# Delta rule block inverses moved from TensorE to GpSimd, with the chunk products four chunks ahead

## What is computed

```
k_beta = k * beta[..., None]; v_beta = v * beta[..., None]
lower = where(strict, einsum('cd,sd->cs', k_beta, k) * decay, 0)
system = lower + eye(C)
sol = triangular_solve(system, [v_beta, k_beta * exp(g)], lower=True)   # u, w
a_qk = where(causal, einsum('cd,sd->cs', q, k) * decay, 0)
step: v_new = u - w @ state
      o = q_dec @ state + a_qk @ v_new
      state = state * exp(g_last) + k_dec.T @ v_new
```

## Time and profile before

| | us |
|---|---|
| median of 3 runs | 2552.06 |
| lowest and highest of the 3 | 2546.36, 2552.57 |
| profiled execution, its own time | 2544.92 |
| its span | 2543.2 |
| where the mix stage lies in the span, about | 697 to 1597 |

### The profile page before, as it was taken

The page is one execution under the profiler, slowest core; times in us unless marked ns, Lnnn a source line. Parts: engine busy times, 40 slices in busy tenths (PEclk is TensorE's granted clock), DMA queues, the critical chain, the costliest instruction groups (busy, mean ns, idle before and its releaser), DMA issues. The chain is left out here.

```text
span 2543.2 us, 47637 instructions
## 1 busy us (share of the span) xinstructions
PE 2318.0 (91%) x17494; PEld 1332.5 (52%) x17495; DVE 1083.7 (43%) x2488; ACT 907.2 (36%) x2283; POOL 389.5 (15%) x630
## 2 busy tenths in 40 slices
PE   6999999999688999999999998799966999999990
PEld 2545545455356666666666666355543444444440
DVE  2434334333346666666666665123344222222223
ACT  2263462633635555555555544111110111111112
POOL 1000000000110000000000000233321222222224
PEclk9999999999879999999999998899987999999995
DMA  9222121111263213211222103733311879999787
GB/s 337 74 66 72 53 79 44 59 59 36 80 171 105 77 54 95 84 55 66 70 70 81 41 27 150 261 120 124 132 67 46 244 210 306 275 322 302 219 238 289
DMA packets 187895, 334.49 MB, mean 132 GB/s; under 512 B 19723, under 2 KB 119718, under 8 KB 184502
## 3 DMA queue, kind: packets, MB, share of 16 engines
q1 hardware_dynamic: 173878, 281.51, 32.4%
q0 software_dynamic: 13824, 50.34, 8.0%
HBM read 242.36 MB, written 89.44 MB: 130 GB/s over the span
## 5 line engine op out<-in xcount | busy, mean ns | idle before, releaser
L706 PE MATMUL pV<-mod_rows_then_work,w_in_sb 128*128 128x512 f32 x768 | 340.1, 596 | 4.3 <-DMA w_in_sb<-in_w_in_dram 4.3
L2077 PE MATMUL hidden_ps<-w,keys_values_then_all 128*128 x752 | 331.6, 594 | 1.1 <-SPq L1949 1.1
L1145 ACT ACTIVATE probs<-scores,neg_max 128x512 f32<-128x512 f32 (+3 forms) x320 | 199.6, 624 | 336.2 <-DVE neg_max L1274 218.5
L1428 PE MATMUL scores<-keys_values_then_all,queries 96*128 96x512 f32 (+3 forms) x640 | 306.9, 563 | 7.2 <-DMA keys_values_then_all<-kp_d 7.2
L2077 PEld LDWEIGHTS hidden_ps<-w,keys_values_then_all 128*128 128x128 f32 x752 | 143.2, 191 | 181.7 <-issue 181.7
L706 PEld LDWEIGHTS pV<-mod_rows_then_work,w_in_sb 128*128 128x128 f32 x768 | 144.4, 191 | 177.2 <-issue 176.4
L1726 PE MATMUL out_ps<-keys_values_then_all 128*128 128x512 f32 x512 | 225.5, 599 | 2.8 <-ACT keys_values_then_all L1591 2.8
L1433 PE MATMUL bank<-ident,probs 128*128 128x128 f32 x1088 | 184.5, 285 | 1.5 <-ACT probs L1145 1.3
L2007 ACT ACTIVATE keys_values_then_all<-hidden_ps 128x256 f32<-128x256 f32 x47 | 18.0, 384 | 455.7 <-PE hidden_ps L2077 455.7
L1274 DVE TENSOR_REDUCE neg_max<-scores 128x1 f32<-128x512 f32 x192 | 132.3, 689 | 111.1 <-PE scores L1428 110.1
L1445 PE MATMUL outT_ps<-probs_T,keys_values_then_all 128*64 128x128 f32 x2176 | 157.8, 284 | 21.6 <-issue 17.6
(11 more groups left out here) (368 smaller groups left out, 3338.0 us busy)
## 6 DMA issues: line engine op xcount, KB each, us to landing
w<-in_w_dram SPq DMA_DIRECT2D x64, 1024.0 KB, 10.1
w_sb<-in_w_dram SPq DMA_DIRECT2D x32, 1024.0 KB, 13.9
w_mod_rows<-in_w_mod_dram SPq DMA_DIRECT2D x16, 1024.0 KB, 4.7
kqv<-qkv_d SPq DMA_DIRECT2D x16, 768.0 KB, 4.3
mod_rows_then_work<-in_w_mod_dram SPq DMA_DIRECT2D x4, 2048.0 KB, 14.7
x_in<-in_x_dram SPq DMA_DIRECT2D x16, 512.0 KB, 4.7
qkv_d<-l_out SPq DMA_DIRECT2D x32, 256.0 KB, 2.3
keys_values_then_all<-y_d SPq DMA_DIRECT2D x16, 512.0 KB, 4.9
```

Of the source, the lines that this page charges most:

```text
L706: last = pe.matmul(pV[n % 2][:], win[:, k, QKV0 + c * P:QKV0 + (c + 1) * P], hT[:, s % 2, k, :], start=(k == 0), stop=(k == ND - 1))
L1145: act.activation(prob[:, e, 0:w].rearrange("p t k -> p (t k)"), pS[e][:, 0:w * P], ACT.Exp, scale=-1.0, bias=nmin[:, i % 2, h, b:b + 1], a ...
L1428: pe.matmul(pS[e][:, 0:w * P], qT[:, i % 2, slot(h)], kT[:, 4 * b:4 * b + w, slot(h), :], start=True, stop=True).then_inc(s_ready, 1)
L2077: last = pe.matmul(pH[par][:], xT[par][:, k], m.w13[:, ds(slot, 1), k].rearrange("p s n -> p (s n)"), start=(k == 0), stop=(k == ND - 1))
```

## The change

The four doubling levels go. In their place GpSimd inverts the 32x32 blocks by forward substitution. The four blocks of each of four heads of two chunks make 32 blocks; each lies on one of the 32 partitions 96 to 127 (in a part of the key buffer that is not used there), row after row in the free dimension. For each column j there is one product of (31 - j) x (j + 1) elements into `outer` and one subtraction from the block of the same size, each waited for before the next: 62 instructions, and two memsets and one transposing copy, for two chunks. They are cut into 16 pieces, steps I, spread over two turns.

The blocks get there by memory: K and KA now write `lt_new` and `at_new`, which SyncE stores (`store_products`), and the blocks are loaded again, a block to a partition (`load_blocks`). At IS the inverses are stored, at L they are loaded into `U`, `Wh` and `Wb`, with `lt` and `at` of that chunk. K and KA run four chunks ahead of the recurrence, with a load `load_kk` of keys and queries alone (512 KB) in one buffer, and `load_kq` loads all of it again for the recurrence. Of the inverse TensorE keeps Y 1, WU 1, Y 2 and WU 2, which are the former 5 and 6. Gates have two buffers in place of three. The block masks (15 GpSimd instructions in the projection and two VectorE reductions at its end) go.

```diff
-    for c in range(-2, NT):
-        n, d = c + 1, c + 2
...
-        steps += [(0.7, ("W0", n)), (0.8, ("Y", n, 1))] * prep
...
+    for c in range(-AHEAD, NT):
+        n, a, d = c + 1, c + AHEAD, c + AHEAD + 1
+        first, prep, rec = a < NT, 0 <= n < NT, c >= 0
+        turn = []
+        turn += [(1.0, ("K", a)), (0.5, ("KA", a))] * first
+        turn += [(0.45, ("VT", c)), (0.45, ("KD", c)), (1.0, ("KS", c)), (0.7, ("QS", c)), (0.85, ("TR", c))] * rec
+        turn += [(0.8, ("Y", n, 1))] * prep
...
+        turn += [(0.5, ("WU", n, 2))] * prep
+        turn += [(0.0, ("G", d))] * (d < NT)
+        turn += [(0.9, ("M", k)) for k in MOD_AT.get(c, ())[-1:]]
+        turn += [(0.0, ("O2", c))] * rec
+        g, half = (c + 3) // BATCH, (c + 3) % BATCH
+        if 0 <= g < NT // BATCH:
+            pieces = [(0.8 if c < 0 else 0.0, ("I", g, k)) for k in range(half * PIECES // 2, (half + 1) * PIECES // 2)]
...
+            turn += [(0.0, ("IS", g))] * half
+        turn += [(0.0, ("L", c + 2))] * (0 <= c + 2 < NT)
+        steps += turn
+    order = [("G", 0), ("K", 0), ("KA", 0), ("G", 1), ("S", 0, 0), ("X", 0, 0), ("S", 0, 1), ("X", 0, 1)]
...
+            def load_blocks(c):
+                wait(lt_stored, 16 * (c + 1))
+                wait(inv_ready, c // BATCH)
+                for q in range(4):
+                    at_row = (c % BATCH * 4 + q) * GH
+                    sp.dma_start(Ab[at_row:at_row + GH], m.a_d[c * P + BL * q:c * P + BL * (q + 1), :].rearrange(
+                        "j (h r i) -> h r j i", h=GH, r=4)[:, q]).then_inc(block_loaded, 16)
...
+            load_kk(0)
...
+            load_kq(0)
             load_kq(1)
             load_gate(0)
-            load_gate(1)
...
+                if kind == "K":
+                    if n + 1 < NT:
+                        wait(kk_ready, n + 1)
+                        load_kk(n + 1)
...
+                elif kind == "IS":
+                    wait(inv_ready, n + 1)
+                    sp.dma_start(m.inv_d[n * (P - QK):(n + 1) * (P - QK), :], both_T).then_inc(inv_stored, 16)
+                elif kind == "L":
+                    load_inverses(n)
...
+            def then(ins):
+                done[0] += 1
+                ins.then_inc(inv_step, 1)
+                pool.wait_ge(inv_step, done[0])
+
+            def invert(g, piece):
...
+                    pool.wait_ge(block_loaded, 16 * 4 * BATCH * (g + 1))
+                for j in range(piece * BL // PIECES, (piece + 1) * BL // PIECES):
+                    below, upto = BL - 1 - j, j + 1
+                    if below:
+                        prod = outer[:, 0:below * upto].rearrange("p (i c) -> p i c", i=below)
+                        then(pool.tensor_tensor(prod, Ab[:, j, j + 1:].unsqueeze(2).to_broadcast([n, below, upto]),
+                                                Tb[:, j:j + 1, 0:upto].to_broadcast([n, below, upto]), ALU.mult))
+                        then(pool.tensor_tensor(Tb[:, j + 1:, 0:upto], Tb[:, j + 1:, 0:upto], prod, ALU.subtract))
+                if piece == PIECES - 1:
+                    pool.tensor_copy(Ub, Tb.rearrange("p i j -> p j i")).then_inc(inv_ready, 1)
...
-                    wait(xw_ready, n * NLV)
+                    wait(lt_stored, 16 * n)
```

More of the change, by code:

```diff
@@ L48 @@
 NEG = -1.0e30
-LVB, BL = 5, 32
+BL = 32
+AHEAD, BATCH = 4, 2
+PIECES = 16
 START = 1
@@ L1091, in _ @@
                     act.copy(R[:], bank[at_bank[step][0]][:]).then_inc(v_copied, 1)
-                elif kind == "W0":
-                    wait(w0_ready, n + 1)
-                    act.copy(WU[:, :, 0], bank[at_bank[step][0]][:, :, 0:BL]).then_inc(w0_copied, 1)
                 elif kind == "Y":
@@ L1105, in _ @@
                         act.copy(Yh[64:], bk[64:, :, 0:64]).then_inc(y_copied, 1)
[L1106 to L1120 removed]
+                elif kind == "WU" and step[2] == 1:
+                    wait(u_ready, NLV * n + 1)
                     wait(xw_ready, NLV * n)
@@ L1350, in _ @@
                     last.then_inc(ks_ready, 1)
-                elif kind == "W0":
-                    wait(u0_ready, n + 1)
-                    for h in range(GH):
-                        for q in quarter:
-                            last = pe.matmul(bank[b0][q, h, 0:BL], WU[q, h, 1], ident_b[q], start=True, stop=True)
-                    last.then_inc(w0_ready, 1)
                 elif kind == "Y":
```

238 lines of the change are left out of this document (106 added, 132 removed).

## The result

| | us |
|---|---|
| before, median of 12 runs | 2551.16 (2546.36 to 2555.65) |
| after, median of 12 runs | 2562.51 (2552.41 to 2566.73) |
| after / before | 1.004, 95% interval 1.0029 to 1.0051 |
| profiled execution of after, its span | 2564.7 (before 2543.2) |

The changed kernel is slower by 0.4%, where 2497 us was predicted. The two profiled executions lie at opposite ends of the runs (2544.9 us of before at the fast end, 2566.4 us of after at the slow end), so that their spans differ by 21.5 us where the medians differ by 11. Page of after: busy time of each engine, the slices of TensorE and its granted clock.

The account below looks back on a forecast made before the run. The prediction took TensorE to bound the mix stage (96% busy in its middle); -80 + 4 + 8 + 7 + 6 + 2 + 5 = -48 us from 2544.9 gave 2497 us, 8 in 10 between 2465 and 2537.

Parts of the forecast that it names:

- Removed on TensorE, -80: Mix stage: 144 small matmul steps (W0, Y, WU) go, saving 75 to 99 us, taken as 80.
- the pauses go too: Rival, chance 0.15: pauses ahead of removed steps vanish as well and the start costs less; 2470 us, 2450 to 2480.
- Added on GpSimd, 43 us a group, hidden: Mix stage: inverting two chunks' blocks takes GpSimd about 43 us of 92 in two turns, hidden behind TensorE.
- limit of 84 us a group: Rival, chance 0.08: GpSimd becomes the bound once a group costs over 84 us; 2630 us at 110 a group.
- Added on the memory path: Mix stage: extra stores and loads hidden; order on SyncE's queue counted nothing, up to 5 us per even turn if GpSimd lags.
- The roots behind the pieces, +2: Mix stage: the output roots queue behind an inversion piece on GpSimd while ScalarE stands at the attention output; 2 us.
- The rest, 4 + 8 + 7 + 6 + 5 = +30: Added costs: M loads 4, start standstill 8, narrow tiles and clock at the start 7, K's decay wait 6, port 5.
- The standstill at K of chunk 1: Start of mix stage: TensorE stands 6 to 10 us for the late load of keys; counted as 8 us.
- The M loads: From turn 8 on: two M about 5 us apart against a 4.7 us load; 4 turns x 1 us, 4 us.
- K's wait for the decay product (+6): Mix stage: G stands close ahead of K, so VectorE waits for GpSimd's mask; 12 turns x 0.5 us.
- The port, +5: Mix stage: VectorE instructions with all tensors in SBUF wait for GpSimd's; 32 us on VectorE, mostly idle time, 5 counted.
- the saving turns into waits: Rival, chance 0.17: waits at K, roots, port and late loads at Y 1 cost 65 us; 2530 us, 2515 to 2537.

Follow-up runs that it names:

- before_small_out: The kernel before without W0 and levels 1 to 4 of Y and WU, with their copies and subtractions (computation left out): 2477.4 us, 0.9705 of before.
- no_block_math: The changed kernel without GpSimd's 62 multiplies and subtractions per group, unit matrices replacing the inverses: 2533.3 us, 0.993 of before.
- roots_no_math: The changed kernel with both roots on ScalarE and the 62 multiplies and subtractions per group left out: 2471.8 us, 0.9694 of before.
- blocks_later: The changed kernel with even chunks' block loads issued behind the store of the previous group's inverses: 2494.5 us, 0.9767 of before.
- root_delta: The changed kernel with only the delta rule's root moved from GpSimd to ScalarE: 2514.3 us, 0.9869 of before.
- root_attn: The changed kernel with only attention's root moved from GpSimd to ScalarE: 2504.5 us, 0.9813 of before.
- later_root_attn: The changed kernel with even block loads behind the store of the inverses and attention's root on ScalarE: 2449.3 us, 0.9599 of before.
- roots_scalar: The changed kernel with both roots, attention's and the delta rule's, moved from GpSimd to ScalarE: 2465.7 us, 0.9658 of before.

## Why the prediction was wrong, point by point

- **Removed on TensorE, -80**: too small. before_small_out gives 76 us as measured and 98 without its longer experts stage (90 to 96 by the mix stage). The sum had counted about 5 of the 24 us of pauses ahead of the steps; the upper end of 99, and the -95 of the rival that the pauses go too, were nearer. That it is the pauses that came free was not shown.
- **Added on GpSimd, 43 us a group, hidden**: the price is right. The groups of after by line:

```profile
L1116 POOL TENSOR_TENSOR keys_values_then_all<-keys_values_then_all 32x31 f32<-32x31 f32 (+15 forms) x248 | 121.0, 488 | 144.7 <-DMA keys_values_then_all<-a_d 124.2 <-POOL attn_rstd L1153 1.2
L1118 POOL TENSOR_TENSOR keys_values_then_all<-keys_values_then_all 32x31 f32<-32x31 f32 (+15 forms) x248 | 132.9, 536 | 19.4
...
L1120 POOL COPY keys_values_then_all<-keys_values_then_all 32x1024 f32<-32x1024 f32 x8 | 15.6, 1953 | 0.5
L1109 POOL MEMSET keys_values_then_all<- 32x1024 f32 x8 | 7.6, 946 | 84.2 <-DMA inv_d<-keys_values_then_all 84.1
```

  (121.0 + 132.9 + 15.6 + 7.6) / 8 = 34.6 us, and 62 times the 0.08 us in front of each (19.4 / 248), 39.5 us. "Hidden" is not right: the arithmetic costs some 50 us with the roots behind it (no_block_math) and 13 to 18 us without (roots_no_math), where the sum had 13 for decay, roots and port together. And the limit of 84 us a group was too high, as it left out the 27 us that a group stands for its transfers.
- **Added on the memory path, "I count nothing, and up to 5 us in each even turn if GpSimd lags"**: this is the step that failed. The text names for `load_blocks` its wait for the store and leaves out the next line, the wait for the inverses of the group before. In the order of the even turn that wait ends only at the turn's end, with KA's position at its start: SyncE's whole queue stands for 31 us in each of 7 turns, where the sum had nothing. Price, by blocks_later: 68 us. That GpSimd does not lag by its work did not matter; it is held in place by the delta root in its own queue (no_block_math, root_delta).
- **The roots behind the pieces, +2**: the mechanism was named and its size was missed, 58 us by root_attn. I had put a root behind one piece (a few us). It stands behind the first piece's wait for its blocks, up to 28.5 us, and then behind several pieces. Together with the queue it is 113 us (later_root_attn), where the sum had 2. The account then reads, from the 2553.5 us of before: -98 removed, +113 for these two, and -6 for all the rest (below), which is what is left over to the measured 2562.5.
- **The rest, 4 + 8 + 7 + 6 + 5 = +30**: with both costs gone the changed kernel is at 2449, 28 us below before_small_out as measured and 6 us below it without the longer experts stage (by the mix stage 797.3 against 803.4 us, also 6), where these terms would have put it 30 above. The standstill at K of chunk 1 was there, about 10 us for the 6 to 10 foretold, but taking it away brought nothing. The M loads cost nothing as long as the queue flows (1.1 and 0.4 us in later_root_attn). K's wait for the decay product (+6) is 2.1 us in all in after, and one standstill of 7 us of TensorE, at 833 us, in roots_scalar and later_root_attn. So something brings back some 36 us against these terms. What it is was not taken apart; the recurrence that starts with more attention ahead of it and the earlier products are candidates.
- **The port, +5**: the contention is there. Its price is not separated: at most the 10 us or so that are left of roots_no_math's 13 to 18. VectorE's gate multiply, first of before, then of after, roots_scalar and roots_no_math:

```profile
L1254 DVE SCALAR_TENSOR_TENSOR gate_in<-q_state_then_out,o_rstd,gate_in 128x128 f32<-128x128 f32 x64 | 18.1, 346 | 1.4 <-POOL o_rstd L1071 1.4
```
```profile
L1292 DVE SCALAR_TENSOR_TENSOR gate_in<-q_state_then_out,o_rstd,gate_in 128x128 f32<-128x128 f32 x64 | 33.7, 585 | 2.2 <-POOL o_rstd L1147 2.2
```
```profile
L1288 DVE SCALAR_TENSOR_TENSOR gate_in<-q_state_then_out,o_rstd,gate_in 128x128 f32<-128x128 f32 x64 | 26.6, 477 | 19.1 <-ACT o_rstd L1214 19.1
```
```profile
L1288 DVE SCALAR_TENSOR_TENSOR gate_in<-q_state_then_out,o_rstd,gate_in 128x128 f32<-128x128 f32 x64 | 22.2, 408 | 19.2 <-ACT o_rstd L1214 19.2
```

  346 to 585 ns beside the pieces, 477 against 408 with and without the arithmetic. By the Trainium skill (SBUF — State Buffer, "Who interferes with whom") a VectorE instruction with two SBUF inputs contends with a GpSimd one that reads SBUF; the durations agree, also where GpSimd's instruction covers 32 partitions only. That it is 408 and not 346 without the arithmetic is not explained by it.
- **The base**: the sum starts from the profiled execution, 2544.9 us, where the median of before is 2551 to 2554. That is 6 to 9 us of the miss.
- **The rivals**: "the saving turns into waits", at 0.17, was the nearest in kind, with 65 us of waits where there were 113; the measured 2562 is above its 2537 too. It was built from K, roots, port and late loads as small terms, not from one queue that stops. Of the prediction's own signs of being wrong three came: Y 1 waiting for its load (13.3 us), G's subtraction above 280 ns (339) and a clock below full in the middle (0.91).

## What to carry to other kernels

For every new wait, write down the line of the queue on which it stands, the step that releases it by its *place in the order* (not by its work), and everything queued behind it: a wait for an event at the end of a turn, placed at the turn's start, costs the whole turn on that queue. Before putting a long or waiting job on an idle engine, look for short steps of the critical path that already live there; here one root of 0.7 us (194 + 548 ns), on an engine that was idle for 75% of the span, cost 58 us. An engine's slack is its idle time less the waits that its new work brings along, and a queue's is none if one entry waits. A run that leaves part of the computation out can change a later stage that depends on the data: here two more blocks of experts, 22 us, made three prices look like others. Compare the untouched stages before you subtract.

## What the runs showed of the hardware

- A standstill is followed by slow matmuls. Of after, around the standstill of TensorE from 824.7 to 842.2 us (columns of the earlier trace rows):

```profile
820.00:825.00 5.00, 4.68 (x54) 2.61 (x51) 2.87 (x8) 2.68 (x11) 0.00 (x0) 1.00 1.14 181
...
845.00:850.00 5.00, 5.00 (x28) 3.71 (x26) 1.67 (x5) 1.50 (x5) 4.45 (x8) 0.50 0.06 14
```

  The granted clock is full (1.00, 2.4 GHz) up to 825 us, half (0.50, 1.2 GHz) from 830 to 850 us and full again from 855 us on. After and later_root_attn have the same 10838 recorded matmuls, yet 2238.9 and 2208.1 us of busy time: 31 us of after's loss are matmuls at a lower granted clock (mean 0.934 and 0.960).
- Short runs on 32 partitions cost GpSimd nothing extra over the rows at 128 partitions (2.12 ns an element). In after the multiply takes 264 ns in the mean for 31 elements and 617 for 256, (617 - 264) / 225 = 1.6 ns an element; the subtraction in place 265 and 728 ns, 2.1 ns. What makes the multiply cheaper was not tried.
- GpSimd's root took 193 + 1026 ns, ScalarE's logarithm and exponential 293 + 205 ns; the shorter pair was nevertheless the dearer place for the delta root, by 17 us (2465.9 against 2449.3).
